# Two layers written out in each engine's program, and a gate round's convolution two chunks later

## The reference, cut to what matters

```python
D_MODEL, SEQ, DEPTH = 4096, 256, 2
for l in range(DEPTH):
    h = rms_norm(x, norm_g[l])
    z = h @ w_in[l]                       # 4096 -> about 9.5 thousand columns, split among four branches
    y_s5  = rms_norm(s5_mixer(s5_u, ...), s5_out_g[l]) * silu(s5_gate)      # diagonal state space, GELU, GLU
    y_mla = rms_norm(mla_mixer(mla_cq, ...), mla_out_g[l]) * silu(mla_gate) # latent attention, 8 heads
    y_gla = gla_mixer(gla_q, ...) * silu(gla_gate)                          # gated linear attention, 4 heads
    y_lru = rms_norm(rglru_mixer(lru_u, ...), lru_out_g[l]) * silu(lru_gate)
    y = concatenate([y_s5, y_mla, y_gla, y_lru], axis=-1)
    x = x + y @ w_out[l]
return rms_norm(x, final_g)

def rglru_mixer(x, ...):                  # the branch whose first step is moved
    xc = causal_depthwise_conv(x, conv_w, width=4) + conv_b
    r = sigmoid(xc @ w_a + b_a); i = sigmoid(xc @ w_x + b_x)      # per block of 128 channels
    log_a = -8 * r * softplus(-lam)
    gated = sqrt(-expm1(2 * log_a)) * (i * xb)
    return linear_scan(exp(log_a), gated)
```

## Time and profile before

| | |
|---|---|
| median of 3 runs | 2826.83 us |
| the profiled execution | 2828.15 us, span 2826.1 us |
| TensorE matmul busy | 2748.5 us, 97% |
| VectorE busy | 2067.6 us, 73% |
| ScalarE busy | 1598.3 us, 57% |
| GpSimd busy | 783.3 us, 28% |
| DMA | 191 GB/s on average |

### The profile page before, as it was taken

The page is one execution under the profiler, slowest core; times in us unless marked ns, Lnnn a source line. Parts: engine busy times, 40 slices in busy tenths (PEclk is TensorE's granted clock), DMA queues, the critical chain, the costliest instruction groups (busy, mean ns, idle before and its releaser), DMA issues.

```text
span 2826.1 us, 56434 instructions
## 1 busy us (share of the span) xinstructions
PE 2748.5 (97%) x15960; PEld 2357.5 (83%) x15960; DVE 2067.6 (73%) x3372; ACT 1598.3 (57%) x2872; POOL 783.3 (28%) x823
## 2 busy tenths in 40 slices
PE   6999999999999999999999999999999999999997
PEld 4888888888888888888878888888888888888886
DVE  8899899866666676555578999997666666855555
ACT  5555555656656575444455555556655656744443
POOL 3255555400110122111134555552010111411111
PEclk9999999999999999999999999999999999999998
DMA  6766666685655657777646565666755555577775
GB/s 217 254 189 175 182 179 187 169 264 168 186 167 167 185 145 218 209 211 209 205 145 209 176 186 175 187 177 189 244 185 165 169 182 165 168 215 212 208 210 176
DMA packets 294196, 538.88 MB, mean 191 GB/s; under 512 B 32432, under 2 KB 43584, under 8 KB 293056
## 3 DMA queue, kind: packets, MB, share of 16 engines
q1 hardware_dynamic: 268736, 497.45, 59.3%
q10 hardware_dynamic: 25344, 39.99, 4.3%
HBM read 516.34 MB, written 25.17 MB: 192 GB/s over the span
## 4 chain that ended last, share of the span: by engine, by line
PE 42%; DVE 3%; issue 3%; ACT 1%; POOL 1%; DVEq 0%; ACTq 0%; POOLq 0%
PE ps L323 26%; PE ps L322 13%; DVE w L1049 1%; PE ps L325 0%; DVE zb L1618 0%; DVE yy L1118 0%; ACT w L626 0%; PE ps L354 0%; DVE g L1112 0%; PE ps L365 0%; POOL lg L1672 0%; ACT half_lo L632 0%; PE ps L342 0%; PE ps L502 0%; PE ps L501 0%
## 5 line engine op out<-in xcount | busy, mean ns | idle before, releaser
L323 PE MATMUL ps<-hb,w 128*128 128x512 f32 x5824 | 2053.1, 396 | 7.4 <-POOL hb L1648 6.1
L1049 DVE TENSOR_TENSOR w<-raw,w 128x512 fp32r<-128x512 f32 x1828 | 1340.2, 743 | 637.9 <-ACT w L626 628.8
L626 ACT ACTIVATE w<-raw 128x512 fp32r<-128x512 f32 x1828 | 1131.2, 629 | 946.6 <-PE ps L323 935.5
L322 PE MATMUL ps<-hb,w 128*128 128x256 f32 x5690 | 1619.4, 285 | 19.7 <-DVE w L1049 18.2
L323 PEld LDWEIGHTS ps<-hb,w 128*128 128x128 f32 x5824 | 1090.9, 188 | 255.9 <-issue 6.7
L322 PEld LDWEIGHTS ps<-hb,w 128*128 128x128 f32 x5690 | 1074.4, 189 | 62.3 <-DVE w L1049 36.1
L323 PE MATMUL ps<-gl,w 128*128 128x512 f32 x800 | 283.5, 395 | 0.0
L1810 POOL TENSOR_TENSOR nf<-zb 128x256 f32 (+1 forms) x60 | 51.9, 865 | 537.2 <-DVE zb L1586 531.6
L322 PE MATMUL ps<-gl,w 128*128 128x256 f32 x680 | 190.3, 280 | 0.0
L323 PE MATMUL ps<-w,hb 128*128 128x512 f32 x512 | 180.7, 396 | 0.0
L323 PEld LDWEIGHTS ps<-gl,w 128*128 128x128 f32 x800 | 149.5, 188 | 30.2
(11 more groups left out here) (312 smaller groups left out, 2416.4 us busy)
## 6 DMA issues: line engine op xcount, KB each, us to landing
raw<-in_w SPq DMA_DIRECT2D x1843, 256.0 KB, 2.8
hd<-heads ACTq DMA_DIRECT2D x16, 512.0 KB, 5.4
gate<-xres ACTq DMA_DIRECT2D x32, 256.0 KB, 4.3
xres<-zb ACTq DMA_DIRECT2D x32, 256.0 KB, 3.6
zb<-in_x SPq DMA_DIRECT2D x8, 512.0 KB, 7.2
xres<-in_x SPq DMA_DIRECT2D x4, 1024.0 KB, 6.6
s5w<-in_s5w ACTq DMA_DIRECT2D x16, 256.0 KB, 3.5
out<-zb SPq DMA_DIRECT2D x4, 1024.0 KB, 3.9
```

Source lines behind the costliest of these rows:

```text
L322: mm(acc[:, T:], a_lo, m_hi, start=False, stop=False, skip_group_check=True)
L323: last = mm(acc, a_hi, m_both, start=(k == 0), stop=(k == nk - 1), skip_group_check=True)
L626: A(w2[:, d, :, 0, :], raw[:, s, :, :], ACT.Copy).then_inc(hi_ready, count)
L1049: V.tensor_tensor(w2[:, d, :, 1, :], raw[:, s, :, :], w2[:, d, :, 0, :].bitcast(F), ALU.subtract).then_inc(w2_ready, count)
```

## The change

The layer loop becomes a Python loop, so that both layers stand one behind the other in the four programs; the loops inside stay. In gate rounds, on ScalarE `inputs` goes from chunk 0 to 2 and `lru_tanh` from 5 to 6; on VectorE the convolution goes from chunks 0 and 1 to 2 and 3, its wait for `pg_ready` with it; on TensorE `mla_scores` and `lru_gates` change places (chunks 5 and 6). In the last round the GLA root goes from chunk 1 to 9 (behind `lru_root`, another Sqrt), its sums from PSUM bank `B_B` to `B_Y`, the reciprocals from 2 to 10, the spread from 7 to 13, the wait for it from 8 to 16, and `y_mul(3)` from 14 to 16.

```diff
-Y_LAST = {5: 0, 8: 1, 11: 2, 14: 3, 21: 4, 22: 5}
+Y_LAST = {5: 0, 8: 1, 11: 2, 16: 3, 21: 4, 22: 5}
-            with pe.Fori(0, L) as l:
+            for l in range(L):                      # likewise on act, dve and pool
-                        columns([(ssq[:, i, :],) for i in (2, 3, 4)], B_B)
+                        columns([(ssq[:, i, :],) for i in (2, 3, 4)], B_Y)
                     def gla_spread():
-                        pe.wait_ge(hf_ready, l * 32 + (16 + 1))
+                        pe.wait_ge(hf_ready, l * 32 + (16 + 3))
-                    steps = {5: [lru_gates], 6: [mla_scores], 9: [gla_gate],      # TensorE
+                    steps = {5: [mla_scores], 6: [lru_gates], 9: [gla_gate],
                     if last:
                         steps[0] = [gla_columns]
-                        steps[7] = [gla_spread]
+                        steps[13] = [gla_spread]
-                    steps = {0: [inputs], 5: [lru_tanh],                          # ScalarE
+                    steps = {2: [inputs], 6: [lru_tanh],
                     if last:
-                        steps[1] = [gla_root, silu_set]
+                        steps[9] = [lru_root, gla_root]
-                    steps = {0: [lambda: conv(1), lambda: conv(2)], 1: [lambda: conv(3)],   # VectorE
+                    steps = {2: [lambda: conv(1), lambda: conv(2)], 3: [lambda: conv(3)],
                     if last:
-                        steps[2] = [lambda: reciprocals(c_l + 4, 6)]
+                        steps[10] = [lambda: reciprocals(c_l + 4, 6)]
                     for c in range(CH_PAIR):
                         if c > 0:
                             lo(n0, c)
-                        if c == 0:
+                        if c == 2:
                             dve.wait_ge(pg_ready, it + 1)
-                        if last and c == 8:
+                        if last and c == 16:
                             dve.wait_ge(rstd_ready, c_l + 4)
```

More of the change, by code:

```diff
@@ L700, in s5_steps @@
                 return steps
-            with act.Fori(0, L) as l:
+            for l in range(L):
                 n_l, h_l, c_l = l * N_LAYER, l * H_LAYER, l * C_LAYER
@@ L956, in gla_root @@
                         act.wait_ge(cols_ready, c_l + 4)
-                        A(ncol[:, 0:6], ps[:, B_B, 0:6], ACT.Sqrt, bias=EPS1, scale=1.0 / (BR // 4)).then_inc(rms_ready, 1)
+                        A(ncol[:, 0:6], ps[:, B_Y, 0:6], ACT.Sqrt, bias=EPS1, scale=1.0 / (BR // 4)).then_inc(rms_ready, 1)
                     if last:
-                        steps[1] = [gla_root, silu_set]
+                        steps[9] = [lru_root, gla_root]
                         for at, p in Y_LAST.items():
@@ L1190, in _ @@
             own.restart()
-            with dve.Fori(0, L) as l:
+            for l in range(L):
                 n_l, h_l, c_l = l * N_LAYER, l * H_LAYER, l * C_LAYER
@@ L1711, in s5_iteration @@
                 own.restart()
-            with pool.Fori(0, L) as l:
+            for l in range(L):
                 h_l, c_l = l * H_LAYER, l * C_LAYER
```

## The result

The changed kernel takes 2808.97 us (median of 4 runs, 2806.02 to 2811.12), the kernel before 2826.92 (4 runs, 2826.18 to 2830.11). The ratio is 0.9934 with an interval of 0.9923 to 0.9946: 18 us, or 0.66%, faster. Forecast were 2814.5 us and a range of 2809.5 to 2821.0. The profiled execution took 2810.84 us (before: 2828.15), its span is 2809.1.

The account below looks back on a forecast made before the run. TensorE's own work plus its gaps was taken as the bound, with only gaps to win: 10.0 + 1.1 + 0.4 + 0.8 = 12.3 us off the median 2826.83 gives 2814.5 us, range 2809.5 to 2821 (8 in 10).

Parts of the forecast that it names:

- The gap at a round's start: Gate rounds 1 to 7, both layers: TensorE's 0.7 us wait for `lo(1)` goes, 10.0 us won.
- The slack of `lo(1)`: Gate round's start: `lo(1)` starts right behind `second_gated` and ends 1.8 us ahead of TensorE's need.
- Chunk 10 had its 2 us: Gate rounds: after the later Tanh, `lo(7)` is ready at 2136.7, TensorE needs it at 2138.7; 2 us left.
- Rival 2: Gate rounds: the gap moves on, paid behind chunk 9; total about 2824; chance 0.10.
- The last round: Last gate round's middle: net 0.4 of 1.8 us per layer won, 0.8 us; bounds 3.6 won or 2 lost.
- Between the layers: Written-out layers drop ScalarE's branch and table load; TensorE's reciprocal wait falls from 1.7 to 0.6, 1.1 us won.
- The clock: Between the layers, 0.60 of full speed, could fall or rise sooner or later: 0, with 1.5 us either way.
- Round 0: Gap at `lo(0)`: fewer register moves ahead of the table load win 0.2 us per layer, 0.4 us; bounds 0 and 2.6.
- Rival 3: VectorE or ScalarE loops: code loading at back edges makes the kernel slower, 2836; chance 0.05.
- Rival 4: Between the layers: nothing gained, as fetching straight code stops TensorE or VectorE; 2815.6; shares the forecast's 0.75.
- Rival 1: More won, all of round 0, the last round and the clock: 18.8 us, so 2808; chance 0.10.

Follow-up runs that it names:

- two operations: The changed kernel with two additions of 512 columns, results unused, on VectorE ahead of `lo(1)` in all gate rounds but the last: 2823.56 us.
- four operations: The changed kernel with four additions of 512 columns, results unused, on VectorE ahead of `lo(1)` in all gate rounds but the last: 2853.24 us.
- one chunk: The changed kernel with inputs, convolution and VectorE's wait for `pg` moved one chunk later than in the kernel before, instead of two: 2810.34 us.
- three chunks: The changed kernel with inputs and convolution three chunks later instead of two, `lru_gates` and `lru_tanh` at chunk 7: 2809.66 us.

## Why the prediction was right in kind and wrong in size

**The gap at a round's start, the term that was mis-sized.** The mechanism was as told: the wait for `pg` over two engines is hidden, and the gap goes in all 14 rounds. But I took its price from the row of idle time, 0.7 us, and it was 0.97; so the term of 10.0 us measured 13.7 (11.80 + 1.94 in the ledger). The rows around the one at 2127.39 in the earlier trace rows hold the rest:

```profile
2126.18 0.28 PE L322 MATMUL ps<-hb,w 128*128 128x256 f32 x1
2126.30 0.39 PE L323 MATMUL ps<-hb,w 128*128 128x512 f32 x1
...
2127.61 0.39 PE L323 MATMUL ps<-hb,w 128*128 128x512 f32 x1
2127.84 0.28 PE L322 MATMUL ps<-hb,w 128*128 128x256 f32 x1
2127.96 0.40 PE L323 MATMUL ps<-hb,w 128*128 128x512 f32 x1
```

Read the starts. Behind an L323 the next matmul starts 0.23 us later (2127.61 to 2127.84), behind an L322 0.12 later (2127.84 to 2127.96). Across the gap it is 2127.39 - 2126.30 = 1.09, so 0.86 late. The matmul after it starts 0.22 behind instead of 0.12, another 0.10. Together 0.96, and the rounds became 0.97 shorter. The idle row leaves out two things: the last matmul before a gap is shown until its modelled end, 0.39 us, though its successor would have started at 0.23 (0.16 hidden), and the first matmul behind the gap takes 0.39 where 0.28 is usual (0.10). The Trainium skill (TensorE: Matmul & The Clock Gate, "Single matmul latency") gives a single bf16 matmul of N columns (398 + N)/2.4 ns at full clock, and the section behind it, "Back-to-back issue gap", gives N/2.4 + 2.5 ns from one to the next. An estimate from these two: a matmul with none behind it takes 163 ns more than its place in the stream. The 0.16 here agrees, but hangs on a modelled end and measures nothing by itself; what is measured is the distance of the starts, which holds both parts.

The runs bear out a constant. Lost by the starts on either side of the gap: 0.97 where 0.70 is shown, 1.08 where 0.81 (two operations), 1.32 where 1.05 (round 0 of the changed kernel), 2.54 where 2.27 (four operations, rounds at full clock). So 0.27 for each gap in the stream, whatever its length. It isn't so at every wait: four L526 start 0.36 us behind the stream without a wait and 0.86 with one, so the 0.47 shown there costs 0.50. For the 14 gaps at round starts the constant is 3.8 us of the 5.3 that the forecast missed in the ledger. It fits what the busy times said: 18 waits fewer in the stream (33 before, 15 now), times 0.27, is 4.9, and "busy" fell by 4.8 for the same matmuls.

**The slack of `lo(1)` was smaller than told.** I had it ready 1.8 us early. The delay by two operations shows 0.83; that by four, 3.07 us of work with 2.27 of gap, shows 0.80. `lo(1)` started 0.83 us behind L1525 instead of at once. Between the two stand the end of the loop's body, its branch and the loop's counters; I had priced them at nothing. The added operation L1562, which waits for no other engine, starts 0.79 us behind L1525 too, so the delay is VectorE's own; how it divides isn't shown. It changed no time, as one chunk is as good as two.

**Chunk 10 had its 2 us.** No wait shows in rounds 1 to 6, and three chunks leave them within 0.03 us. Rival 2 is excluded, with a chunk to spare.

**The last round was the second mis-sized term:** 0.8 forecast, 2.9 measured. Two errors. I read "three waits, 1.8 us" as its middle, but the first of them, 0.74 at 9.19 us into the round, is the round's start, already counted among the seven; the middle had two, 0.66 + 0.39 = 1.05. And of these I took 0.4 as won, because I set doubtful steps against each other. Both went, which is 1.05 + 2 x 0.27 = 1.59, and 0.23 more at chunk 18, where no row shows idle time. Against that stand 0.50 for the new wait at L526, about 0.1 at chunk 22, and 0.2 that the spread costs more behind chunk 13 than behind chunk 7. That makes 1.0; the round's middle was shortened by 1.13 and 1.18 (2.10 and 2.15 less 0.97), and the rest is in steps too small to place. Behind the round 0.31 more came.

**Between the layers** 1.1 was forecast and 1.24 measured in this execution, by the step named: reciprocal's wait 0.6, no branch, no load. The clock, for which I had kept 1.5 us either way, did move. Executions of the same changed kernel, windows from 1400 to 1424, first the one shown above, then two of the later ones:

```profile
1400.00:1424.00 24.00, 17.43 (x77) 14.70 (x76) 14.55 (x28) 10.12 (x19) 9.24 (x7) 0.72 0.29 93
```

```profile
1400.00:1424.00 24.00, 17.40 (x83) 14.32 (x82) 15.42 (x29) 11.12 (x20) 9.46 (x8) 0.79 0.34 102
```

```profile
1400.00:1424.00 24.00, 17.44 (x85) 14.50 (x85) 14.74 (x28) 10.85 (x19) 8.41 (x7) 0.79 0.34 102
```

The granted clock is 0.72 of full speed in the first and 0.79 in the others, and they gain 2.36 and 2.46 us here instead of 1.24. So two executions of one kernel differ here by as much as the term itself. Of the twelve traces with written-out layers two show 1.24 (the first, and the one with the table loads put back), the others 1.76 to 2.46; the new order alone, with the loop, shows no gain. Whether writing out has a part in the shorter time at half clock isn't shown; two traces with the loop, this one and the kernel before, are too few.

**Round 0** gave 0.85 where 0.4 was told. Its idle time fell from 1.29 to 1.05 in each layer; the new order alone gave 0.19 per layer, the written-out layers alone 0.24, so both parts have a share and my reason (fewer register moves) covers only one.

**Rival 3** is excluded for this layout: in the changed kernel's trace neither ScalarE nor VectorE is idle for more than 0.9 us at an inner branch, and the written-out program in the old order is not slower. Rival 4 is out too, since the stretch between the layers did gain. Rival 1 gave the right time, 2808, for the wrong reasons: of its terms the last round's 3.6 is close to the 2.9 (4.9 with the round's start), but round 0 gave a third of its 2.6, and the clock gave nothing in the execution that the ledger reads. Its price of a gap was the same 0.7.

**What stays open:** the input rounds of the second layer lost 1.18 us net in this execution, 0.84 of it in the first, where matmuls still ran at half clock; the rest are steps of half a microsecond that come and go between executions of one kernel. I know where they are, not what makes them.

## What to carry to other kernels

Price a gap of TensorE by the starts of the matmuls on either side of it, against their usual distance, not by the idle time that its row shows: each break in the stream of L322 and L323 cost 0.27 us more, which matters when gaps are under a microsecond and there are dozens. When one order of work comes up in every round, put the operation that waits for other engines behind those that TensorE is about to need; one chunk did it, and two or three changed rounds 0 to 6 by at most 0.04 us. A loop over two halves of a program, written out, was worth 1.2 to 2.5 us at its one pass between the layers by the traces, below what the 11 runs of it alone could tell; count where the branch stands in a chain before doing it.

## What the runs showed of the hardware

- A gap in TensorE's stream of 256- and 512-column fp32r matmuls costs a constant on top: 0.70 shown cost 0.97, 0.81 cost 1.08, 1.05 cost 1.32, 2.27 cost 2.54.
- TensorE came back at half clock behind 7 of 14 gaps of 1.9 to 2.3 us (granted clock 0.51 over 3.42 us in the one read), which cost 1.2 to 1.6 us each time. Behind none of the gaps of 0.70 or 0.81 did it fall.
- ScalarE's stop at the outer loop's branch took 2.68 us, and the two table loads of 1.28 us that follow in a program without it are hidden in ScalarE's wait for TensorE.
